# Gate and up weights fetched two k-steps at a time, as 8 KB per partition, in a hybrid encoder kernel

## What is computed

```
h = rmsnorm(x, norm_ffn_g)
logits = h @ w_router                       # (1024, 16)
aff = softmax(logits)
gate, tok = top_k(aff.T, 128)               # per expert
xin = h[tok]                                # 128 x 2048
a, u = xin @ w_gate[e], xin @ w_up[e]       # 2048 x 1024 each
y = (silu(a) * u) @ w_down[e]               # 1024 x 2048
out = rmsnorm(x + scatter_add(gate * y), final_norm_g)
```

## Time and profile before

| | |
|---|---|
| median of 3 runs | 2655.34 us (2655.18 to 2656.62) |
| the profiled execution's own time | 2652.87 us |
| its span, first to last instruction | 2651.1 us |
| mean granted TensorE clock | 0.995 |
| PE busy | 2607.4 us, 98% |
| DVE busy | 2154.1 us, 81% |
| ACT busy | 1509.5 us, 57% |
| POOL busy | 599.5 us, 23% |
| moved by DMA | 872.61 MB, mean 329 GB/s, 269094 packets |

### The profile page before, as it was taken

The page is one execution under the profiler, slowest core; times in us unless marked ns, Lnnn a source line. Parts: engine busy times, 40 slices in busy tenths (PEclk is TensorE's granted clock), DMA queues, the critical chain, the costliest instruction groups (busy, mean ns, idle before and its releaser), DMA issues.

```text
span 2651.1 us, 33753 instructions
## 1 busy us (share of the span) xinstructions
PE 2607.4 (98%) x12165; PEld 2152.5 (81%) x12165; DVE 2154.1 (81%) x2706; ACT 1509.5 (57%) x1765; POOL 599.5 (23%) x862
## 2 busy tenths in 40 slices
PE   9999999999999999999999999999999999999996
PEld 7888888887888888878878788888888888888884
DVE  7775776479888866867766899999999999999987
ACT  6433221122232256874344478888888888888776
POOL 1432111221111153840113311111112121211002
PEclk9999999999999999999999999999999999999998
DMA  9688876899999978516677699999999999999998
GB/s 365 237 295 295 289 253 230 277 344 358 403 378 391 344 227 274 186 62 198 212 249 262 252 373 388 410 407 401 406 406 403 405 403 405 402 406 403 401 400 366
DMA packets 269094, 872.61 MB, mean 329 GB/s; under 512 B 32118, under 2 KB 57221, under 8 KB 246029
## 3 DMA queue, kind: packets, MB, share of 16 engines
q1 hardware_dynamic: 221664, 705.06, 69.5%
q0 software_dynamic: 47264, 165.40, 17.7%
HBM read 747.83 MB, written 125.08 MB: 329 GB/s over the span
## 4 chain that ended last, share of the span: by engine, by line
PE 88%; DMA 4%; DVE 2%; ACT 2%; SPq 1%; issue 1%; POOL 1%; POOLq 0%; DVEq 0%; ACTq 0%
PE ps L3584 26%; PE ps L3192 5%; PE ps L3193 5%; PE ps L3194 5%; PE ps L3615 4%; PE ps L3614 4%; PE ps L3613 4%; PE ps L3188 4%; PE ps L3190 4%; PE ps L3189 4%; PE ps L3422 4%; PE ps L3424 4%; PE ps L3423 4%; PE ps L3243 1%; PE ps L3131 1%
## 5 line engine op out<-in xcount | busy, mean ns | idle before, releaser
L3021 DVE SCALAR_TENSOR_TENSOR elo<-eraw,mixg,ehi 128x2048 fp32r<-128x2048 f32 x256 | 597.9, 2348 | 51.3 <-ACT ehi L2013 44.4
L2013 ACT ACTIVATE ehi<-eraw,mixg 128x2048 fp32r<-128x2048 f32 x256 | 512.8, 2012 | 130.8 <-PE ps L3584 91.1
L1621 ACT ACTIVATE whi<-raw 128x1024 fp32r<-128x1024 f32 x159 | 168.7, 1061 | 574.9 <-DVE raw L2127 264.9
L3584 PE MATMUL ps<-ehi,xh 128*128 128x512 f32 x960 | 375.1, 391 | 0.0
L3584 PE MATMUL ps<-elo,xh 128*128 128x512 f32 x960 | 373.7, 389 | 0.0
L2132 DVE TENSOR_TENSOR wlo<-raw,whi 128x1024 fp32r<-128x1024 f32 x159 | 194.4, 1222 | 154.0 <-ACT whi L1621 153.4
L3024 DVE TENSOR_TENSOR elo<-eraw,ehi 128x2048 fp32r<-128x2048 f32 x128 | 293.6, 2313 | 16.4 <-ACT ehi L2015 13.5
L2015 ACT ACTIVATE ehi<-eraw 128x2048 fp32r<-128x2048 f32 x128 | 243.8, 1918 | 60.5 <-PE ps L3615 34.9
L3584 PE MATMUL ps<-ehi,xl 128*128 128x512 f32 x960 | 256.6, 389 | 0.0
L3584 PEld LDWEIGHTS ps<-ehi,xl 128*128 128x128 f32 x960 | 180.2, 188 | 37.5
L3584 PEld LDWEIGHTS ps<-ehi,xh 128*128 128x128 f32 x960 | 180.2, 188 | 37.2
(11 more groups left out here) (522 smaller groups left out, 5819.0 us busy)
## 6 DMA issues: line engine op xcount, KB each, us to landing
raw<-in_w_stream SPq DMA_DIRECT2D x271, 512.0 KB, 6.8
eraw<-in_w_gate SPq DMA_DIRECT2D x256, 512.0 KB, 7.8
eraw<-in_w_up SPq DMA_DIRECT2D x256, 512.0 KB, 9.8
eraw<-in_w_down SPq DMA_DIRECT2D x128, 1024.0 KB, 11.1
wsum<-in_w_stream SPq DMA_DIRECT2D x64, 256.0 KB, 7.0
scr_w_sums<-wsum POOLq DMA_DIRECT2D x16, 1024.0 KB, 9.4
scr_x<-oxs POOLq DMA_DIRECT2D x64, 256.0 KB, 3.9
oraw<-scr_w_sums SPq DMA_DIRECT2D x64, 256.0 KB, 2.6
```

The source lines that it names most:

```text
L2013: act.activation(ehi[:, p % ERING, :], raw_, ACT.Copy, scale=mixg[:, k:k + 1]).then_inc(S["e_hi"], 1)
L3021: dve.scalar_tensor_tensor(out=elo[:, p % ERING, :], in0=raw_, scalar=mixg[:, k:k + 1], in1=ehi[:, p % ERING, :].bitcast(F32), op0=ALU.mul ...
L3584: last = pe.matmul(gu_bank(e, c), a[:, k, :], w[:, p % ERING, c * BW:(c + 1) * BW], start=(k == 0 and a is hi and w is ehi), stop=(k == KD ...
```

## The change

Two k-steps of gate and up form a couple. The slot of the even step of a couple now holds 256 rows of `w_gate`, the slot of the odd step the same 256 rows of `w_up`. In such a load partition p gets rows 2p and 2p+1 of the 256, which lie next to each other in memory, so 8 KB per partition in one DMA of 1 MB. What k-step k then reads is one half of either slot (`raw_pair_of`): gate from the even step's slot, up from the odd step's slot, as two pieces of 1024 elements that lie 8 KB apart in a partition. The k order follows from it: k-step k has rows 2p + (k mod 2) of its 256 rows. So PE's transposes of the tokens read every second element of a 256-wide piece of `xg`, and the norm weights for the experts are loaded once more in that order (`g_exp`) after the router has used theirs.

The turns of the semaphores follow: `pair_high` of a gate and up step waits for both slots of the couple; `fetch_pair` into a slot that an even gate and up step had waits for DVE to be done with the odd step too; each slot's semaphore now counts 16 per load. All instructions that read or write `ehi` and `elo` in `pair_high` and `pair_low` are given as two halves.

```diff
-LANDED = [sum(32 if PAIRS[q][0] == "gu" else 16 for q in range(p % EDEEP, p + 1, EDEEP)) for p in range(NP)]
+LANDED = [16 * (p // EDEEP + 1) for p in range(NP)]
...
+        def raw_pair_of(p):
+
+            (kind, _, k), q = PAIRS[p], p % EDEEP
+            if kind == "d":
+                return eraw[:, 2 * q:2 * q + 2, :]
+            first = 2 * (q - k % 2) + k % 2
+            return eraw[:, first:first + 3:2, :]
+
+        def halves_of(a):
+
+            return a.rearrange("p (a c) -> p a c", a=2)
...
                 if p >= EDEEP:
-                    sp.wait_ge(S["e_lo"], p - EDEEP + 1)
+                    before = p - EDEEP
+                    sp.wait_ge(S["e_lo"], before + 2 if PAIRS[before][0] == "gu" and before % 2 == 0 else before + 1)
                 if p == FIRSTS:
                     sp.wait_ge(S["gathered"], BEFORE["gathered"] + 16)
                 kind, e, k = PAIRS[p]
-                q, rows = p % EDEEP, slice(k * P, (k + 1) * P)
+                q = p % EDEEP
                 if kind == "gu":
-                    sp.dma_start(eraw[:, 2 * q, :], t["w_gate"][e, rows, :]).then_inc(ersem[q], 16)
-                    sp.dma_start(eraw[:, 2 * q + 1, :], t["w_up"][e, rows, :]).then_inc(ersem[q], 16)
+                    src = t["w_up" if k % 2 else "w_gate"][e, (k - k % 2) * P:(k - k % 2 + 2) * P, :].rearrange("(p r) c -> p (r c)", r=2)
                 else:
-                    sp.dma_start(flat2(eraw[:, 2 * q:2 * q + 2, :]), t["w_down"][e, rows, :]).then_inc(ersem[q], 16)
+                    src = t["w_down"][e, k * P:(k + 1) * P, :]
+                sp.dma_start(flat2(eraw[:, 2 * q:2 * q + 2, :]), src).then_inc(ersem[q], 16)
...
+                if q == 9 * KO:
+                    sp.wait_ge(S["r_scaled"], BEFORE["r_scaled"] + 1)
+                    sp.dma_start(mixg[:, :], t["g_exp"]).then_inc(S["gain_in"], 16)
...
             def pair_high(p):
 
-                act.wait_ge(ersem[p % EDEEP], ER0[p % EDEEP] + LANDED[p])
+                kind, _, k = PAIRS[p]
+                for slot in (p - k % 2, p - k % 2 + 1) if kind == "gu" else (p,):
+                    act.wait_ge(ersem[slot % EDEEP], ER0[slot % EDEEP] + LANDED[slot])
                 if p >= ERING:
                     pair_used(act, p - ERING)
-                raw_, (kind, _, k) = flat2(eraw[:, 2 * (p % EDEEP):2 * (p % EDEEP) + 2, :]), PAIRS[p]
                 if kind == "gu":
-                    act.activation(ehi[:, p % ERING, :], raw_, ACT.Copy, scale=mixg[:, k:k + 1]).then_inc(S["e_hi"], 1)
+                    act.activation(halves_of(ehi[:, p % ERING, :]), raw_pair_of(p), ACT.Copy, scale=mixg[:, k:k + 1]).then_inc(S["e_hi"], 1)
                 else:
-                    act.activation(ehi[:, p % ERING, :], raw_, ACT.Copy).then_inc(S["e_hi"], 1)
+                    act.activation(halves_of(ehi[:, p % ERING, :]), raw_pair_of(p), ACT.Copy).then_inc(S["e_hi"], 1)
...
+            act.wait_ge(S["gain_in"], 64)
...
-                    last = pe.transpose(x_bank(e, g)[:, j * P:(j + 1) * P], xg[:, k * P:(k + 1) * P], ident[:, :])
+                    last = pe.transpose(x_bank(e, g)[:, j * P:(j + 1) * P], xg[:, (k - k % 2) * P + k % 2:(k - k % 2 + 2) * P:2], ident[:, :])
...
+        "g_exp": norm_ffn_g[0].reshape(KD // 2, P, 2).transpose(1, 0, 2).reshape(P, KD),
```

More of the change, by code:

```diff
@@ L3018, in pair_low @@
                 dve.wait_ge(S["e_hi"], p + 1)
-                raw_, (kind, _, k) = flat2(eraw[:, 2 * (p % EDEEP):2 * (p % EDEEP) + 2, :]), PAIRS[p]
+                kind, _, k = PAIRS[p]
+                low, high = halves_of(elo[:, p % ERING, :]), halves_of(ehi[:, p % ERING, :]).bitcast(F32)
                 if kind == "gu":
-                    dve.scalar_tensor_tensor(out=elo[:, p % ERING, :], in0=raw_, scalar=mixg[:, k:k + 1],
-                                             in1=ehi[:, p % ERING, :].bitcast(F32), op0=ALU.mult, op1=ALU.subtract).then_inc(S["e_lo"], 1)
+                    dve.scalar_tensor_tensor(out=low, in0=raw_pair_of(p), scalar=mixg[:, k:k + 1], in1=high,
+                                             op0=ALU.mult, op1=ALU.subtract).then_inc(S["e_lo"], 1)
                 else:
-                    dve.tensor_tensor(elo[:, p % ERING, :], raw_, ehi[:, p % ERING, :].bitcast(F32), ALU.subtract).then_inc(S["e_lo"], 1)
+                    dve.tensor_tensor(low, raw_pair_of(p), high, ALU.subtract).then_inc(S["e_lo"], 1)
             def x_low(e, g):
```

## The result

| | before | change |
|---|---|---|
| median of 22 runs each | 2654.36 us (2652.01 to 2656.62) | 2658.43 us (2656.13 to 2665.39) |
| ratio, 95% interval | | 1.0017 [1.0012, 1.0023] |
| the profiled execution's own time | 2652.87 us | 2662.66 us |
| its span | 2651.1 us | 2660.9 us |
| PE, DVE, ACT busy | 2607.4, 2154.1, 1509.5 us | 2612.3, 2153.7, 1509.2 us |

The time lies inside the range, 3.1 us above the forecast. But no change was forecast, and the interval of the ratio excludes 1: the change costs about 4 us. The profiled execution of the change is 4.2 us above its own median, so its stages are compared by distances within them.

The account below looks back on a forecast made before the run. PE was taken to bound the experts' stage, busy 1086.00 of 1086.00 us, with loads running ahead. All terms summed to 0 on 2652.87 us; for the median the forecast was 2655.3 us, range 2651 to 2661 us.

Parts of the forecast that it names:

- Transposes that read every second element: PE's 256 token transposes, with no idle time to cover them: bounded between 0 and 28 us, taken as 0.
- The middle value of 59 ns: Token transposes on PE: weight load reading at half pace adds 59 ns each, 256 times, 15 us.
- The rival: PE pays for stepped transposes: 15 us, up to 28 us, deciding from 21 ns per transpose; chance 0.08.
- Later issue, earlier need: Gate and up loads into even steps' slots issued up to 2.7 us later, even step needing both slots; 0.
- the 3.4 us of reserve: Tightest couple of loads: 19.3 us from issue to split, slowest landing 15.9 us, so 3.4 us left.
- Fewer issues: SP's 256 pairs of loads become single ones: up to 125 us less of SP's time, 0 on the path.
- bigger pieces: Gate and up loads of 1 MB with 8 KB per partition: rate 2.6% better, 0 on the path.
- split instructions in two pieces: ACT and DVE work on two pieces of 1024 elements: 2.7 us on DVE, covered by idle time; 0.
- two slots at the start: ACT's first splits wait for two slots; loads there by 1502.2 us, splits start at 1511.47; 0.
- the gain load: One more load (`g_exp`) in the block before the experts: some 0.4 us of SP's time, 0.
- no gain from memory: Rejects the rival that memory set the pace of gate and up steps: 18 us faster, 2637 us, chance 0.04.

Follow-up runs that it names:

- step of four: Kernel before with token transposes alone reading every fourth element (16 bytes), output that of permuted tokens: 2656.97 us, +2.7, ratio 1.0010.
- three steps later: Kernel before with the change's later waits before loads, and every turn of the ring three steps (8.2 us) later still: 2661.85 us, +7.0, ratio 1.0025.
- late turns alone: Kernel before with only the change's wait in `fetch_pair`, loading an even gate and up step's slot after the odd step: 2657.03 us, +2.7, ratio 1.0011.
- the mended kernel: Against the kernel before: host-laid couples for experts 0 to 13, flat transposes, fetches and turns of before in 14 and 15: 2654.97 us, +1.3, ratio 1.0006.
- the gain load alone: Kernel before with only the fourth norm weight load added, the same weights fetched again and ACT waiting for it: 2655.30 us, +0.5, ratio 1.0001.
- the couples without the step and the gain load: The change with weights laid out by the host, flat transposes and no `g_exp`: 2657.01 us against 2654.28 us for the kernel before, ratio 1.0011.

## Why the prediction was wrong

*Where it failed first: "Transposes that read every second element", taken as 0.* The mechanism was named, with its place and the right argument that PE has no cover, and then priced at 0 by the row "it is nearest to", with a rule of the Trainium skill to support it (the section is named under the step of four). Measured: 12.4 ns for each, 3.2 us in all, between the bounds of 0 and 28 us. The middle value of 59 ns was a good estimate of the weight load itself (+69 ns, 140 to 209), and the remark that part of it would lie under other work was right; it is no reason for 0. From the earlier trace rows, a transpose took 111 ns; now a group of eight takes 1.42 - 2 x 0.227 = 0.97 us, 121 ns each. (These 10 ns and the 12.4 by the scatters differ by 0.02 us per group, no more than the rounding of the four starts to 0.01 us can make.) So most of the load's 69 ns lie beside other work; how the overlap is divided within a group the trace doesn't tell. The rival had the mechanism right, its price (15 us) five times too high, and its threshold of 21 ns was not reached. The threshold was too high as well: it took 5.3 us for the least that can be told, and 22 runs of each kernel told 4. What was missing was a case between 0 and 21 ns, and since this term could only add, it had to move the forecast.

*Where it failed second: "Later issue, earlier need. ... So 0".* The path from issue to need was reckoned rightly: 19.3 us for the last couple, and in the profile it is 19.3 (issued 1934.19, split 1953.46); the slowest landing was put at 15.9 us and was 15.1. No slot ran dry, and three steps later none did either, so the 3.4 us of reserve were reckoned too small. But the only question put was whether a split comes too late. The step did not ask who else stands in the queue when the loads are done. The statement that "what is full there is a queue that SP fills ahead of need" holds up to the last scatter, not behind it. The earlier trace rows has only a stage from 2620 us on there, share 0.71 with the idle end mixed in; the window from 2550.68 to 2635.68 at 427 GB/s and the last store's 5.4 us in the chain of before would have shown it. It costs about 2 us: 1.8 in the change's profile, 2.5 with late turns alone.

*The range.* That the time still lies in it is luck of size: the range left 5.3 us above the forecast for what a measurement can't tell, and two costs that were both taken as 0 happened to be smaller than that together. And the forecast started from 2655.34 us, the median of 3 runs, where 22 runs gave 2654.36: this hides 1 us of the miss.

*How the two add.* 3.2 and 1.8 us make 5.0 by the profiles; the ratio gives 4.5 us (0.0017 x 2654), its interval 3.2 to 6.1. Singly the parts measured +3.9 and +2.7, each with an interval of some 2.4 us to either side, which is too wide to say whether they add in full.

*Right.* Fewer issues 0, bigger pieces 0, split instructions in two pieces 0 (ACT 2013 ns and DVE 2348 ns at the median, before 2013 and 2347), two slots at the start 0, the gain load 0, and no gain from memory (the mended kernel). The packets fell by 36,720 on SP's queue where 32,000 were forecast: 256 x 128 from the pieces, and 3,952 more, which is 256 x 16 less 144 for the gain load, as if each DMA brought 16 small ones of its own. Two other runs bear this out: the gain load alone adds 144 packets (128 + 16), and the couples without the step and the gain load have 36,864 fewer on that queue (256 x 144). The Trainium skill's wish for at least 1 MiB per DMA ("DMA: Bandwidth & Descriptors", "Rules for kernel authors") gave nothing here: in the experts' stage no one waits for a load.

## What to carry to other kernels

A DMA share of 1.0 can mean two things: a queue filled ahead of need, in which lateness is free, or the last stretch before the end, in which every byte not yet moved is paid at the rate of that stretch (here 427 GB/s, so 1 MB is 2.3 us). So a change that issues loads later is priced at the end of the kernel as well, by bytes still to move there, and not only by asking who waits in the steady stage. And on an engine without idle time an unpriced term that can only add is not 0: take a small price and say so.

## What the runs showed of the hardware

- A float32 stationary operand of 128 columns read with a step loads in 209 ns instead of 140; steps of 2 and 4 cost the same (209 and 211 ns at the median). On PE's path only 12.4 ns of it appear where eight such transposes follow each other.
- A load's time to landing is not fixed: with all turns three steps later, issue to need of the last couple fell from 19.3 us to 11.8 us, and the loads there landed in at most 10.5 us instead of up to 12.4 in the change.
- With PE setting the pace, the distance between experts repeats to 2 ns: 68.206 to 68.208 us in the ten profiles without the step, 68.406 and 68.407 in the four with it. That resolves 12 ns per transpose, where the medians of the runs don't.
